# A hybrid recurrent/gating block on one core: three engine lists of its recurrent units in another order, and two weight sums made earlier on POOL

## The chip, the cores and the metric

The kernel runs on one core of one Trainium2 chip. The metric is the device time of one execution in microseconds; 1542.42 us is the median of three executions before the change (1542.19 to 1542.64).

## The reference

One layer over a sequence of 1024 tokens with 1024 channels (batch 1), all in fp32:

```python
h = modulated_rmsnorm(x, g, shift1, scale1)
xr, gr, zu, zv, ga, gb = split(h @ w_in)                  # six times 1024 columns
xr = causal_dwconv(xr, rnn_conv_w, rnn_conv_b)            # 4 taps
r = sigmoid(block_diag(xr, w_a) + b_a)                    # 8 heads of 128 x 128
i = sigmoid(block_diag(xr, w_x) + b_x)
log_a = 8 * r * log_sigmoid(lam);  a = exp(log_a)
u = sqrt(-expm1(2 * log_a)) * (i * xr)
hs = scan(h_t = a_t * h_t-1 + u_t)                        # along the sequence
y_a = (hs * gelu(gr)) @ w_branch_a
y_b = (gelu(zu) * position_mix(layernorm(gelu(zv)))) @ w_branch_b
x = x + gate1 * ((sigmoid(ga) * y_a + sigmoid(gb) * y_b) @ w_out)
h = modulated_rmsnorm(x, g2, shift2, scale2)              # then up-projection, conv(3), gelu(a)*b,
x = x + gate2 * (ffn(h) @ w_down)                         # down-projection, and a last rmsnorm
```

## The kernel before

**Units.** The work is a list `SEQ` of units, each of which makes two tiles of 128 x 1024 in PSUM (a "value" and an "activation" tile). The list begins G0, G1 (gates), then R0 to R7 (the recurrent units, one for each head), ZV0 to ZV3, G2 to G7, ZU0 to ZU3, and then the branches, the output projection and the channel sub-layer. `pos` is a unit's place in the list: R0 to R7 are pos 2 to 9, ZV0 and ZV1 are pos 10 and 11. The change touches the loops over pos 2 to 19.

**Products.** Most units are computed by a Strassen-like scheme with seven products instead of eight: b11, t1, t2, b22, t3, b21 and t4, in this order on TensorE (L807, called from `unit`). Each product is 12 matmuls of 128 x 128 by 128 x 512, because an fp32 operand is split into a high and a low part of fp32r and three partial products are taken. After the fourth product of pos, the block-diagonal matmuls of the recurrent unit before it (L930, 12 matmuls) go between.

**Weight operands.** Op n of a unit (n0 to n0+6 in the order A11, S1, S2, S4, S3, A12, A22) is the weight side of one product. A11, A21, A22 and A12 are loaded from HBM by the SP queue into `raw` buffers; POOL makes four of the seven operands in `weight_sums`: S1 = A21 + A22 (L649), S3 = A11 - A21 (L652), S2 = S1 - A11 (L656), S4 = A12 - S2 (L660). S1 needs a free buffer, which it gets when the low part of op n0+5 of the unit before is made. S2 overwrites A11 and so waits for the low part of op n0, and S4 overwrites S1 and waits for that of op n0+1. ScalarE then copies the operand to its high part (`hi`, L1221), VectorE subtracts to get the low part (`lo`, L1834), and the product waits for `lo` (semaphore f_lo). Loads of A21 and A22 of the next unit reuse buffers that `lo(n0+3)` of this unit frees.

**Snapshots and joins.** ScalarE copies three PSUM banks aside in a unit (`snap`, L1236, after products b11, t1 and t2), because the next product goes onto the same bank; VectorE adds them back (`join` 0, 1, 2, L1848). Product t2 waits for snap 0, b22 for snap 1, t3 for snap 2, and t4 for joins 0 and 1.

**A recurrent unit m** is finished while the products of the two units after it run. In the unit right after it: ScalarE starts the convolution (`conv_start`, L1354, still at the end of the unit itself), VectorE does three more taps (`conv`, L2011) and the low part of the block-diagonal weights (L2019), ScalarE takes the gelu (L1362) and the high part of the convolved tile (`conv_high`, L1374), VectorE its low part (`conv_low`, L2024), then TensorE does the block-diagonal product. `gate_pair` (L1382, L1387) takes the two tanh, `decay` a tanh, an exp and a square (L1394, L1398, L1403), and VectorE `gated_input` (L2029). There is one buffer `la_a` for the decay: the first tanh of unit m waits until the scan of unit m-1 has been done. In the unit after that: `decay_square` (L2034, VectorE), `decay_root` (L1407, ScalarE), `scan_input` and `scan` (L2039, L2043, VectorE), and the product with the gelu gate on POOL (L667), whose result SP stores.

**Order.** Each engine runs its own list, written out by hand as a loop over pos and seven steps w in a unit. An engine works its list strictly in order, and a wait holds up all that stands behind it. ScalarE's and VectorE's lists work on `hi(n0+w+3)` and `lo(n0+w+3)` at step w, so in steps 4 to 6 they make the first operands of the next unit: n0+7, n0+8, n0+9 are the next unit's A11, S1 and S2.

Of the kernel before, what the change touches and what calls it, by code (L numbers as in the profile page):

```python
# [17 lines left out]
def build(nc, a, out):  # L18
# [16 lines left out]
    CW = a["rnn_conv_w"].shape[1]  # L35
# [37 lines left out]
    with ExitStack() as ctx:  # L73
# [558 lines left out]
        @block.gpsimd  # L632
        def _(pool):
            nc.gpsimd.memset(ident[:, :], 0.0).then_inc(consts_made, 1)
            pool.wait_ge(consts_made, 1)
            nc.gpsimd.affine_select(out=ident[:, :], in_=ident[:, :], compare_op=ALU.not_equal, fill=1.0, base=0,
                                    pattern=[[-1, P]], channel_multiplier=1).then_inc(consts_made, 1)
            nc.gpsimd.memset(ones[:, :], 1.0).then_inc(consts_made, 1)

            def weight_sums(item, parts=(0, 1)):  # L640
                n0, at = first_op[item], s_slots[item]
                made = 4 * block_unit[item]
                a11, a21, a22, a12, s1 = (raw[at[x][0]][:, 0:depth[n0], :] for x in ("A11", "A21", "A22", "A12", "S1"))
                if 0 in parts:
                    if at["S1"][1] is not None:
                        pool.wait_ge(f_lo, at["S1"][1] + 1)
                    pool.wait_ge(at["A21"][1], at["A21"][2])
                    pool.wait_ge(at["A22"][1], at["A22"][2])
                    nc.gpsimd.tensor_tensor(s1, a21, a22, ALU.add).then_inc(s_made, 1)  # L649
                    pool.wait_ge(at["A11"][1], at["A11"][2])  # L650
                    pool.wait_ge(s_made, made + 1)
                    nc.gpsimd.tensor_tensor(a21, a11, a21, ALU.subtract).then_inc(s_made, 1)  # L652
                if 1 in parts:
                    pool.wait_ge(f_lo, n0 + 1)
                    pool.wait_ge(s_made, made + 2)
                    nc.gpsimd.tensor_tensor(a11, s1, a11, ALU.subtract).then_inc(s_made, 1)  # L656
                    pool.wait_ge(f_lo, n0 + 2)
                    pool.wait_ge(at["A12"][1], at["A12"][2])
                    pool.wait_ge(s_made, made + 3)
                    nc.gpsimd.tensor_tensor(s1, a12, a11, ALU.subtract).then_inc(s_made, 1)  # L660

            for pos in range(2, AT["A", 0]):
                weight_sums(SEQ[pos])
                m = prev_unit(pos, "R", 2)
                if m is not None:
                    pool.wait_ge(scanned, m + 1)
                    nc.gpsimd.tensor_tensor(ti[m % 2][:, :], ti[m % 2][:, :], gg[m % 2][:, :], ALU.mult).then_inc(y_ready, 1)  # L667
                if SEQ[pos] == ("ZV", 0):
                    pool.wait_ge(ws_landed, 16)
                    nc.gpsimd.affine_select(out=ws_raw[:, :, :], in_=ws_raw[:, :, :], compare_op=ALU.is_ge, fill=0.0, base=0,  # L670
                                            pattern=[[0, G], [-1, P]], channel_multiplier=1).then_inc(ws_masked, 1)

            weight_sums(("O", 2))

            for pos in range(NF + PLAIN, len(SEQ) - 1):
                if SEQ[pos][0] != "M":
                    weight_sums(SEQ[pos])


            for i in range(2 * KT - 1):  # L680
                h = i // KT
                pool.wait_ge(sqf_ready, i + 1)
                if i % KT == 0:
                    pool.wait_ge(sum_lo, IN_LO + O_PARTS + 4)
                    nc.gpsimd.tensor_copy(qf[:, H[h]], sqf[i % 4][:, :]).then_inc(qf_added, 1)
                else:
                    pool.wait_ge(qf_added, i)
                    nc.gpsimd.tensor_tensor(qf[:, H[h]], qf[:, H[h]], sqf[i % 4][:, :], ALU.add).then_inc(qf_added, 1)
# [524 lines left out]
        def _(act):  # L1213
# [176 lines left out]
            def decay(m, weights, n):  # L1390
                act.wait_ge(gates_read, 2 * m + 1)
                if m:
                    act.wait_ge(m2_ready, m)
                nc.scalar.activation(th[:, :], la_a[:, :], ACT.Tanh, bias=la4n[:, m:m + 1],  # L1394
                                     scale=la4n[:, m:m + 1]).then_inc(ach, 1)
                weights(n)
                act.wait_ge(ach, 2 * m + 1)
                nc.scalar.activation(la_a[:, :], la_a[:, :], ACT.Exp, bias=la4[:, m:m + 1],  # L1398
                                     scale=la4[:, m:m + 1]).then_inc(ach, 1)
                act.wait_ge(ach, 2 * m + 2)  # L1400
                if m:
                    act.wait_ge(tail_step, m)
                nc.scalar.activation(m2[:, :], la_a[:, :], ACT.Square).then_inc(th_ready, 1)  # L1403

            def decay_root(m):
                act.wait_ge(m2_ready, m + 1)
# [59 lines left out]
            for pos in range(2, AT["A", 0]):  # L1466
# [2 lines left out]
                m, m_past = prev_unit(pos, "R"), prev_unit(pos, "R", 2)  # L1469
                b = V_BLOCK[pos] if pos in V_BLOCK else None  # L1470
                for w in range(7):
                    if w in (1, 2, 3):
                        snap(pos, w - 1)
                    if m is not None and w == 2:
                        conv_high(m)
                    if w == 0:
                        if m is not None:
                            block_diag_high(m)
                        elif pos > 2:
                            OUT[SEQ[pos - 1][0]](pos - 1, 1)  # L1480
                        if SEQ[pos] == ("G", 2):
                            stage(0)
# [336 lines left out]
        def _(dve):  # L1819
# [184 lines left out]
            lo(10)  # L2004


            def conv(m, banks):
                x, src = xc[m % 2], flat(banks[0])
                dve.wait_ge(tap0, m + 1)
                for d in range(1, CW):  # L2010
                    tap = V.scalar_tensor_tensor(x[:, d:S], src[:, 0:S - d], C("rnn_conv_w", (CW - 1 - d) * KT + m), x[:, d:S],  # L2011
                                                 ALU.mult, ALU.add)
                    if d < CW - 1:
                        step(tap)
                tap.then_inc(conv_done, 1)

            def block_diag_low(m):
# [68 lines left out]
            for pos in range(2, AT["A", 0]):  # L2086
# [3 lines left out]
                b = V_BLOCK[pos] if pos in V_BLOCK else None  # L2090
                past = BANKS[(pos - 1) % 2]
                for w in range(7):
                    if w >= 4:
                        join(pos, w - 4)
                    if m is not None and w == 5:
                        gated_input(m)
                    if m is not None:
                        if w == 0:
                            conv(m, past)
                            block_diag_low(m)  # L2100
                        if w == 1:
                            conv_low(m)
                    if m_past is not None and w == 1:
                        decay_square(m_past)
                    if m_past is not None and w == 3:
                        scan_input(m_past)
                        scan(m_past)
# [19 lines left out]
                    if item == ("ZU", 3):  # L2127
                        for k in ((), (), (), (0, 1), (2, 3), (), (4, 5))[w]:
                            ya_low(k)
                    lo(n0 + w + 3)  # L2130


            def ada_piece(e, k):
# [562 lines left out]
```

## Time and profile before

| | |
|---|---|
| median of three executions | 1542.42 us |
| the profiled execution's own time | 1542.83 us |
| its span, first to last instruction | 1540.8 us |
| TensorE busy | 1516.1 us (98%), 6820 matmuls |
| VectorE busy | 1222.6 us (79%) |
| ScalarE busy | 811.0 us (53%) |
| POOL busy | 381.7 us (25%) |
| granted TensorE clock | 1.000 in the whole span |
| pos 4 to pos 11 (R2 to ZV1) on TensorE | 125.83 to 304.73 us |

Times are in microseconds from the first instruction. "Busy" is the time in which an engine has an instruction under way; matmuls are pipelined, so a busy TensorE can still be held up a little between two of them. Weight loads (PEld) show the pace better: each matmul has one.

### The profile page before, as it was taken

The page shows a single profiled execution, that of the slowest core. Times are in us where ns is not written, and L with a number is a line of the kernel's source. Part 1 is how long each engine was busy: PE and PEld are TensorE (multiplying, and loading weights), DVE is VectorE, ACT ScalarE, POOL GpSimd, SP SyncE. Part 2 cuts the span into 40 slices and gives each one's busy share as a digit, 9 for nine tenths or more (in the row PEclk, how much of TensorE's full clock was granted, in tenths as well). Part 3 has the DMA queues.
Part 4 walks back from the last instruction along what each step waited for, and adds up shares of the span by engine and source line. Part 5 has one row for each costly group of instructions (what it writes and reads, how often), then busy time and mean ns, then how long its engine had stood idle before and what let it go on. Part 6 is the DMA issues. An engine that isn't in the chain of part 4 may idle for free.

```text
span 1540.8 us, 19510 instructions
## 1 busy us (share of the span) xinstructions
PE 1516.1 (98%) x6820; PEld 1241.4 (81%) x6820; DVE 1222.6 (79%) x1484; ACT 811.0 (53%) x1207; POOL 381.7 (25%) x291
## 2 busy tenths in 40 slices
PE   7999999999999999999999999999999999999998
PEld 4778777788888888888887788888888888888887
DVE  6987988745656685478868999999999987778786
ACT  5368888645555461012534555555555553444447
POOL 0023434422222200000010333333333331233224
PEclk9999999999999999999999999999999999999999
DMA  9532222312332347574421144444444446677722
GB/s 347 180 105 60 89 69 79 96 55 82 106 103 66 110 150 233 181 246 146 164 62 35 48 150 161 154 150 150 151 151 151 150 130 229 229 242 252 238 89 110
DMA packets 199984, 219.56 MB, mean 142 GB/s; under 512 B 8944, under 2 KB 155728, under 8 KB 199120
## 3 DMA queue, kind: packets, MB, share of 16 engines
q1 hardware_dynamic: 199888, 218.32, 42.8%
q8 instruction: 55, 0.90, 0.2%
q14 instruction: 41, 0.34, 0.1%
HBM read 160.61 MB, written 57.67 MB: 142 GB/s over the span
## 4 chain that ended last, share of the span: by engine, by line
PE 76%; DVE 15%; ACT 4%; issue 3%; DMA 1%; POOL 0%; SPq 0%; ACTq 0%; DVEq 0%; POOLq 0%
PE ps L807 57%; PE ps L880 10%; DVE wop L1834 4%; DVE hidw L2466 1%; PE ps L1158 1%; PE ps L1067 1%; PE ps L1010 1%; PE ps L1140 1%; DVE ps L1848 1%; PE ps L965 1%; DVE part_acc L1897 1%; ACT wop L1221 1%; DVE yq L1932 1%; DVE tn L1927 1%; DVE ti L2039 1%
## 5 line engine op out<-in xcount | busy, mean ns | idle before, releaser
L1221 ACT ACTIVATE wop<-raw 128x512 fp32r<-128x512 f32 (+1 forms) x529 | 299.8, 570 | 419.2 <-PE ps L807 162.0
L1834 DVE TENSOR_TENSOR wop<-raw,wop 128x512 fp32r<-128x512 f32 (+1 forms) x529 | 385.5, 736 | 165.1 <-ACT wop L1221 161.8
L807 PE MATMUL ps<-yq,wop 128*128 128x512 f32 x1680 | 405.2, 390 | 1.3 <-DVE wop L1834 0.7
L807 PEld LDWEIGHTS ps<-yq,wop 128*128 128x128 f32 x1680 | 314.3, 188 | 71.2 <-issue 3.9
L649 POOL TENSOR_TENSOR raw<-raw,raw 128x512 f32<-128x512 f32 (+1 forms) x65 | 96.4, 1483 | 863.3 <-DVE wop L1834 377.5
L807 PE MATMUL ps<-dq,wop 128*128 128x512 f32 x840 | 191.3, 389 | 0.5 <-DVE wop L1834 0.5
L807 PEld LDWEIGHTS ps<-dq,wop 128*128 128x128 f32 x840 | 157.4, 188 | 34.2 <-issue 1.2
L807 PE MATMUL ps<-t4q,wop 128*128 128x512 f32 x528 | 128.5, 392 | 2.0 <-DVE ps L1848 1.9
L807 PE MATMUL ps<-t2q,wop 128*128 128x512 f32 x528 | 127.7, 391 | 1.8 <-DVE wop L1834 1.0
L807 PE MATMUL ps<-t3q,wop 128*128 128x512 f32 x528 | 127.9, 391 | 0.8 <-ACT snap_u L1236 0.8
L807 PE MATMUL ps<-t1q,wop 128*128 128x512 f32 x528 | 127.7, 391 | 0.0
L1848 DVE TENSOR_TENSOR ps<-ps,snap_p 128x512 f32<-128x512 f32 x128 | 88.8, 694 | 47.3 <-PE ps L807 46.6
L2466 DVE SCALAR_TENSOR_TENSOR hidw<-ps,pc,hidw 128x1023 f32<-128x1023 f32 x96 | 122.5, 1277 | 0.9
L1236 ACT ACTIVATE snap_p<-ps 128x512 f32<-128x512 f32 x128 | 76.3, 596 | 83.2 <-PE ps L807 82.8
L807 PEld LDWEIGHTS ps<-t4q,wop 128*128 128x128 f32 x528 | 98.2, 188 | 26.6 <-DVE ps L1848 6.5
L807 PEld LDWEIGHTS ps<-t2q,wop 128*128 128x128 f32 x528 | 98.8, 188 | 23.7 <-ACT snap_p L1236 3.1
L807 PEld LDWEIGHTS ps<-t3q,wop 128*128 128x128 f32 x528 | 98.4, 188 | 21.5 <-ACT snap_u L1236 1.2
L807 PEld LDWEIGHTS ps<-t1q,wop 128*128 128x128 f32 x528 | 98.5, 188 | 20.1
L656 POOL TENSOR_TENSOR raw<-raw,raw 128x512 f32<-128x512 f32 (+1 forms) x65 | 79.6, 1224 | 75.3 <-DVE wop L1834 71.0
L660 POOL TENSOR_TENSOR raw<-raw,raw 128x512 f32<-128x512 f32 (+1 forms) x65 | 75.6, 1163 | 78.9 <-DVE wop L1834 73.9
L652 POOL TENSOR_TENSOR raw<-raw,raw 128x512 f32<-128x512 f32 (+1 forms) x65 | 88.0, 1354 | 9.3
L880 PE MATMUL ps<-ya_split,wop 128*128 128x512 f32 x384 | 87.8, 390 | 0.0
(266 smaller groups left out, 1978.9 us busy)
## 6 DMA issues: line engine op xcount, KB each, us to landing
dq<-hid_keep SPq DMA_DIRECT2D x35, 1024.0 KB, 7.3
raw<-in_w_in SPq DMA_DIRECT2D x96, 256.0 KB, 3.3
raw<-in_w_up SPq DMA_DIRECT2D x96, 256.0 KB, 3.3
hid_keep<-part_b SPq DMA_DIRECT2D x40, 512.0 KB, 3.0
ada_ring<-in_w_ada SPq DMA_DIRECT2D x32, 512.0 KB, 4.6
hid_keep<-part_t SPq DMA_DIRECT2D x20, 512.0 KB, 2.8
raw<-in_w_down SPq DMA_DIRECT2D x80, 128.0 KB, 2.4
ada_w<-in_w_ada SPq DMA_DIRECT2D x8, 1024.0 KB, 11.5
```

The lines of the kernel that those rows point to most:

```text
L649: nc.gpsimd.tensor_tensor(s1, a21, a22, ALU.add).then_inc(s_made, 1)
L652: nc.gpsimd.tensor_tensor(a21, a11, a21, ALU.subtract).then_inc(s_made, 1)
L656: nc.gpsimd.tensor_tensor(a11, s1, a11, ALU.subtract).then_inc(s_made, 1)
L660: nc.gpsimd.tensor_tensor(s1, a12, a11, ALU.subtract).then_inc(s_made, 1)
L807: done = nc.tensor.matmul(bank, left[:, w, lk, :], right[:, x, rk, :], start=(first and w == 0 and x == 0), stop=(last and w == 1), skip_g ...
L880: done = nc.tensor.matmul(psum[:, h, :], wop[n % 4][:, w, k % KH, :], right(k, x, h), start=(k == 0 and w == 0 and x == 0), stop=(k == KT ...
L965: last = nc.tensor.matmul(blocks(past[1])[:, g, :], vhat[:, g, :], wsT[:, g, :], start=True, stop=True)
L1221: nc.scalar.activation(wop[n % 4][:, 0, 0:depth[n], :], raw[slot][:, 0:depth[n], :], ACT.Copy).then_inc(f_hi, 1)
L1236: nc.scalar.activation(dst[:, :], src, ACT.Copy).then_inc(snapped, 1)
L1834: V.tensor_tensor(wop[n % 4][:, 1, 0:kd, :], raw[slot_of[n][0]][:, 0:kd, :], wop[n % 4][:, 0, 0:kd, :].bitcast(F32), ALU.subtract).then_in ...
L1848: V.tensor_tensor(out_b, in_b, kept[:, :], ALU.add).then_inc(joined, 1)
L2466: tap = V.scalar_tensor_tensor(dst[:, d:S], src[:, 0:S - d], C("ffn_conv_w01" if k < 2 else "ffn_conv_w2", k % 2 * 2 * FT + f), dst[:, d:S ...
```

## The change

Four things change in the loops over pos 2 to 19:

- POOL: while recurrent units are in flight, S1 and S3 of the next unit are made before the gate product (L667) of this step instead of after it.
- ScalarE, `decay`: `hi(n0+8)` stands behind the square instead of between tanh and exp.
- ScalarE, unit ZV1 alone: snapshot 0 stands before the second gelu of ZV0 instead of two instructions behind it.
- VectorE, where a recurrent unit precedes: `lo(n0+3)` stands between the second and the third of the convolution's taps; joins 0 and 1 stand together ahead of `lo(n0+7)`; join 2 stands ahead of `lo(n0+8)`; `decay_square(m)` is moved from step 1 of the next unit to step 6 of this one, between `lo(n0+8)` and `lo(n0+9)`.

```diff
             for pos in range(2, AT["A", 0]):
-                weight_sums(SEQ[pos])
                 m = prev_unit(pos, "R", 2)
+                weight_sums(SEQ[pos], (1,) if prev_unit(pos, "R", 3) is not None else (0, 1))
                 if m is not None:
+                    weight_sums(SEQ[pos + 1], (0,))
                     pool.wait_ge(scanned, m + 1)
                     nc.gpsimd.tensor_tensor(ti[m % 2][:, :], ti[m % 2][:, :], gg[m % 2][:, :], ALU.mult).then_inc(y_ready, 1)
...
                 nc.scalar.activation(th[:, :], la_a[:, :], ACT.Tanh, bias=la4n[:, m:m + 1],
                                      scale=la4n[:, m:m + 1]).then_inc(ach, 1)
-                weights(n)
                 act.wait_ge(ach, 2 * m + 1)
                 nc.scalar.activation(la_a[:, :], la_a[:, :], ACT.Exp, bias=la4[:, m:m + 1],
                                      scale=la4[:, m:m + 1]).then_inc(ach, 1)
...
                 nc.scalar.activation(m2[:, :], la_a[:, :], ACT.Square).then_inc(th_ready, 1)
+                weights(n)
...
                 for w in range(7):
-                    if w in (1, 2, 3):
+                    if w in (1, 2, 3) and (w > 1 or SEQ[pos] != ("ZV", 1)):
                         snap(pos, w - 1)
...
                     if w == 0:
+                        if SEQ[pos] == ("ZV", 1):
+                            snap(pos, 0)
...
-            def conv(m, banks):
+            def conv(m, banks, weights, n):
                 x, src = xc[m % 2], flat(banks[0])
                 dve.wait_ge(tap0, m + 1)
                 for d in range(1, CW):
+                    if d == CW - 1:
+                        weights(n)
+                        dve.wait_ge(vch, middle)
                     tap = V.scalar_tensor_tensor(x[:, d:S], src[:, 0:S - d], C("rnn_conv_w", (CW - 1 - d) * KT + m), x[:, d:S],
                                                  ALU.mult, ALU.add)
-                    if d < CW - 1:
+                    if d < CW - 2:
                         step(tap)
+                    elif d == CW - 2:
+                        middle = step_number(tap)
                 tap.then_inc(conv_done, 1)
...
                 for w in range(7):
-                    if w >= 4:
+                    if w == 4 or w >= 4 and m is None:
                         join(pos, w - 4)
-                    if m is not None and w == 5:
-                        gated_input(m)
                     if m is not None:
+                        if w == 4:
+                            join(pos, 1)
+                        if w == 5:
+                            gated_input(m)
+                            join(pos, 2)
+                        if w == 6:
+                            decay_square(m)
                         if w == 0:
-                            conv(m, past)
+                            conv(m, past, lo, n0 + 3)
                             block_diag_low(m)
                         if w == 1:
                             conv_low(m)
-                    if m_past is not None and w == 1:
-                        decay_square(m_past)
...
-                    lo(n0 + w + 3)
+                    if w or m is None:
+                        lo(n0 + w + 3)
```

## Rows read from the trace of the kernel before

**Rows 1.** The page: the span and the chain that ended last.
```profile
span 1540.8 us, 19510 instructions
...
PE 76%; DVE 15%; ACT 4%; issue 3%; DMA 1%; POOL 0%; SPq 0%; ACTq 0%; DVEq 0%; POOLq 0%
```

**Rows 2.** Timeline of the weight loads: start, length, operation, [idle before].
```profile
192.60 2.68 PEld L807 LDWEIGHTS ps<-yq,wop 128*128 128x128 f32 x12
195.32 2.68 PEld L807 LDWEIGHTS ps<-t1q,wop 128*128 128x128 f32 x12
...
201.28 2.58 PEld L807 LDWEIGHTS ps<-yq,wop 128*128 128x128 f32 x12 [0.56 <-issue]
...
212.47 2.59 PEld L807 LDWEIGHTS ps<-t4q,wop 128*128 128x128 f32 x12 [0.45 <-DVE ps L1848]
215.10 2.68 PEld L807 LDWEIGHTS ps<-yq,wop 128*128 128x128 f32 x12
...
290.57 2.61 PEld L807 LDWEIGHTS ps<-t2q,wop 128*128 128x128 f32 x12 [1.06 <-ACT snap_p L1236]
...
302.05 2.63 PEld L807 LDWEIGHTS ps<-t4q,wop 128*128 128x128 f32 x12 [0.71 <-DVE ps L1848]
```

**Rows 3.** Timeline of ScalarE in the unit at pos 7.
```profile
195.89 0.63 ACT L1221 ACTIVATE wop<-raw 128x512 fp32r<-128x512 f32 x1
...
200.27 1.06 ACT L1374 ACTIVATE xc_split<-xc 128x1024 fp32r<-128x1024 f32 x1
...
203.75 1.06 ACT L1407 ACTIVATE m<-m 128x1024 f32<-128x1024 f32 x1 [0.61 <-DVE m L2034]
...
208.44 1.12 ACT L1382 ACTIVATE la_a<-ps,hba 128x1024 f32<-128x1024 f32 x1 [0.80 <-DVE ti L2043]
...
212.99 0.63 ACT L1221 ACTIVATE wop<-raw 128x512 fp32r<-128x512 f32 x1 [1.30 <-POOL raw L649]
...
214.79 1.06 ACT L1403 ACTIVATE m<-la_a 128x1024 f32<-128x1024 f32 x1
216.39 1.21 ACT L1354 ACTIVATE xc<-ps,pc 128x1024 f32<-128x1024 f32 x1 [0.54 <-DVE ps L1848]
```

**Rows 4.** Timeline of VectorE in the same unit.
```profile
196.33 3.90 DVE L2011 SCALAR_TENSOR_TENSOR xc<-ps,pc,xc 128x1023 f32<-128x1023 f32 x3
...
201.36 1.23 DVE L2024 TENSOR_TENSOR xc_split<-xc,xc_split 128x1024 fp32r<-128x1024 f32 x1 [0.19 <-ACT xc_split L1374]
202.50 1.22 DVE L2034 SCALAR_TENSOR_TENSOR m<-m,th 128x1024 f32<-128x1024 f32 x1
203.64 1.29 DVE L1834 TENSOR_TENSOR wop<-raw,wop 128x512 fp32r<-128x512 f32 x2
...
204.85 1.23 DVE L2039 TENSOR_TENSOR ti<-ti,m 128x1024 f32<-128x1024 f32 x1
206.11 2.29 DVE L2043 TENSOR_TENSOR_SCAN ti<-la_a,ti 128x1024 f32<-128x1024 f32 x1
...
209.50 2.30 DVE L1834 TENSOR_TENSOR wop<-raw,wop 128x512 fp32r<-128x512 f32 x1
...
211.73 0.69 DVE L1848 TENSOR_TENSOR ps<-ps,snap_p 128x512 f32<-128x512 f32 x1
212.33 1.70 DVE L2029 SCALAR_TENSOR_TENSOR ti<-ti,xc 128x1024 f32<-128x1024 f32 x1
213.96 1.78 DVE L1834 TENSOR_TENSOR wop<-raw,wop 128x512 fp32r<-128x512 f32 x1
```

**Rows 5.** Timeline of POOL in the same unit.
```profile
208.48 2.78 POOL L667 TENSOR_TENSOR ti<-ti,gg 128x1024 f32<-128x1024 f32 x1 [12.62 <-DVE ti L2043]
...
213.10 2.10 POOL L652 TENSOR_TENSOR raw<-raw,raw 128x512 f32<-128x512 f32 x1
...
217.06 1.29 POOL L660 TENSOR_TENSOR raw<-raw,raw 128x512 f32<-128x512 f32 x1 [0.17 <-POOL raw L656]
```

**Rows 6.** The page's DMA issues: count, size, us to landing.
```profile
raw<-in_w_in SPq DMA_DIRECT2D x96, 256.0 KB, 3.3
```

## The prediction

> **What bounds the kernel now.** I read the page first. The span is 1540.8 us and TensorE holds three quarters of the chain that ended last [rows 1]: the kernel is a row of products, and a change pays only where a product is made to wait. So I went to the weight loads of TensorE over pos 3 to 12. Two products follow each other at 2.72 us where nothing holds them [rows 2], so the eight products of a recurrent unit could take 8 x 2.72 = 21.76 us. From pos 5 to pos 10 a unit takes 22.50 us (192.60 to 215.10 [rows 2]; the other five lie within 0.05 of it). The 0.74 us come from two waits that the reader sees there: b22 starts late at 201.28, waiting for its low weights, and t4 at 212.47, waiting for join 1. At ZV1 (pos 11) t2 waits 1.06 us for snapshot 0 and t4 0.71 us for join 1 [rows 2]. All that lists can win here is thus 6 x 0.74 = 4.4 us and some 2 us in ZV1, about 6.5 us or 0.4%.
>
> Next I asked why the waits are the same in each unit: something goes round with a period of 22.50 us. The timeline of ScalarE shows it. The first tanh of unit m waits for the scan of unit m-1 (0.80 us idle at 208.44 [rows 3]); from that tanh the list runs on without a rest through exp, square, conv_start, gelu, conv_high and root, the root releases scan_input and scan, and the scan the next tanh. This **loop** sets the period, not TensorE. Four idle times lie on it [rows 3]: 1.30 us before hi(n0+8) (it waits for S1 from POOL, and the exp is queued behind it), 0.54 before conv_start (join 2), 0.61 before the root (decay_square), and the scan itself.
>
> The timelines of VectorE and POOL show one more thing: the two engines stop each other. `lo` takes 0.69 us alone (two of them in a row 1.29 at 203.64), but 2.30 at 209.50, beside POOL's gate product, and 1.78 at 213.96 beside S3 [rows 4, 5]. Both end 0.54 us after the POOL instruction (211.80 against 211.26, 215.74 against 215.20): a held `lo` begins 0.15 before POOL is done. It works the other way too: S3 takes 2.10 instead of 1.29, ending 1.17 after gated_input (214.03) [rows 4, 5]. And it goes by turns: the `lo` at 213.96 was ready when gated_input ended, but S3 had stood waiting and went first. The join at 211.73, which has one operand in PSUM, keeps its 0.69 beside S1.
>
> **The change, part by part.** I follow the loop once round. Let s be the end of the square.
>
> *Taken out of the loop.* hi(n0+8) no longer stands in front of the exp, so its 1.30 goes. Join 2 is ahead of lo(n0+8) and done long before conv_start: 0.54 goes. decay_square is done a unit earlier, so the root runs as soon as its table is there: 0.61 goes. Together 2.45 us. Also b22 gets lo(n0+3) one tap earlier, and t4 gets join 1 ahead of the `lo` that the gate product held (2.30). If nothing else happened, the loop would be 20.05 us, and TensorE with 21.76 would set the pace.
>
> *S4 behind decay_square.* hi(n0+8) now starts at the end of the square (s - 0.10) and ends at s + 0.53; lo(n0+8) ends at s + 1.26. S4 overwrites S1 and waits for just this `lo`. But decay_square is next on VectorE, its square is done, and it starts before POOL has seen the semaphore: it runs from s + 1.17 to s + 2.39, and S4 ends 1.17 later, at s + 3.56. ScalarE comes to hi(n0+3), which copies S4, at s + 2.43: conv_start at s + 0.43, and 2.00 from there (216.39 to 195.89 + 22.50 [rows 3]). It waits 1.17 us. If S4 went first this would shrink to 0.2, but decay_square would push the taps back by as much, so the sum with the next item stays between 1.7 and 2.0.
>
> *The taps.* lo(n0+9) is held by S4 and ends 0.54 after it, s + 4.10. The three taps take 3.90 and lo(n0+3) among them another 0.60 [rows 4]: the convolution ends at s + 8.5. ScalarE would be at conv_high 4.38 after hi(n0+3) [rows 3], at s + 7.98. It waits 0.58 us. Behind it stand hi(n0+5) and the root. The new wait inside the convolution (for hi(n0+3), done at s + 4.2, two taps before its turn) costs nothing.
>
> *S1 ahead of the gate product.* Let x be the end of conv_high (201.33 [rows 3]). conv_low follows at once, then, with decay_square gone from here, the two `lo`: lo(n0+5) ends at x + 2.46 (0.03 + 1.14 + 1.29 [rows 4]). It frees S1's buffer and POOL starts S1 0.08 later (the lag of 208.48 behind the scan's end [rows 4, 5]); 1.29 long, it ends at x + 3.83. The loads are there: lo(n0+3) frees their buffers at s + 7.2, and 3.3 us [rows 6] later, s + 10.5, is 1.6 before S1's turn. scan_input is ready at x + 2.91 (the root starts at 203.75 - 0.61 = x + 1.81, takes 1.06). It finds S1 at work and starts at x + 3.68: 0.77 us late.
>
> *S3 ahead of the scan.* S3 has queued meanwhile and by turns goes next: scan_input ends at x + 4.91, S3 at x + 6.08, and the scan starts at x + 5.93 instead of x + 4.94: 0.99 us late. No row shows the scan beside POOL. Its price is between 0 (if it is not held) and 0.99; of the rows, it is nearest to gated_input, also 1024 long with both operands in SBUF, which was held. I take 0.99. [...]
>
> *Sum.* 22.50 - 2.45 + 1.17 + 0.58 + 0.77 + 0.99 = 23.56 us: the loop becomes longer by about 1.0 us a unit, since the two sums that POOL now makes early fall just on scan_input and scan, the only place in the loop where VectorE works alone. TensorE's waits move: t2 late for snapshot 0, b22 for snapshot 1, t4 for join 1.
>
> The loop must first eat the lead that the cuts give at its start: pos 4 stays at 21.8, pos 5 gains 0.3 over its 22.50; pos 6 to 10 lose 5 x 1.0. In ZV1 the early snapshot saves the 1.06, but t4 waits for join 1, behind scan, S3 and the product: 1.0 and about 1.3 later. Between -1.1 (the sums come after the scan) and +2.3 I take +0.4. Total 0.3 + 5.0 + 0.4 = 5.7 us. On the profiled execution (1542.83, 0.4 above the median) that is 1548.5; on the median **1548.1 us**, 0.37% slower. A change of 0.2% (3.1 us) is about what a measurement here can tell from none.
>
> **Rivals.** *1. The scan is not held by POOL.* Place: L2043 beside L652; price 0.99 a unit; it decides if the scan's mean stays at 2.29. Then the loop is 22.6, as before, but starts with its lead: about 1 us won in the first two units, perhaps 0.2 in each later one, and 1.1 in ZV1: 3 us faster, 1539.4. For it: no row shows the scan held. Against: every two-operand SBUF instruction beside POOL is. 14%.
>
> *2. S1 comes later than scan_input* (by late loads, or because the two, 0.37 apart, change places). Then S1 holds the scan alone, 1.0 instead of 1.76, and S3 comes after it; the gate product is later, in no one's way until the next sums. The loop is 22.8, ZV1 wins 0 to 1: +1 to +3.5 us, about 1544.7. Against: a margin of 1.6 us for the loads. 15%.
>
> *3. The lists do all they can:* no collision, TensorE sets the pace at 21.76; 6.5 us faster, 1536. It needs three of the four new waits to be wrong. 4%.
>
> *4. Worse:* the S1/S3 lag goes on into join 0 and 1 and the loads: 24 a unit, 1551 or more. 6%.
>
> **How the numbers follow.** The forecast (1545.5 to 1550.5, which lets the new waits sum to 2.9 to 3.7 and ZV1 go either way) has 61%. Rival 1 lies on the border and goes half to faster, half to same; rival 2 half to same, half to slower. Faster: 7 + 4 and some for what I have not seen, 16%. Same: 7 + 8 and some, 17%. Slower: 67%. The range takes in rival 2 and the upper part of rival 1: 1540.0 to 1550.5.
>
> **What the changed profile would show.** Right: weight loads of b11 about 23.4 apart from pos 6 to 10; scan_input at a mean near 2.0 instead of 1.23 and the scan near 3.2 instead of 2.29; S1 starting 0.1 after lo(n0+5); ScalarE idle some 1.1 before hi(n0+3), waiting for L660, and some 0.5 before conv_high; no idle time before exp or root; t4 of ZV1 waiting some 2 to 3 us. Wrong: a scan of 2.29 with S3 under it, S1 starting behind scan_input, or a period at or under 22.5.

## The result, and the profile after

The changed kernel takes 1548.27 us (median of five, 1544.93 to 1550.04), the kernel before 1542.42 (five, 1541.86 to 1542.64). The ratio is 1.0035, 95% interval 1.0025 to 1.0046: 5.9 us slower. (Three executions of 2182 to 3364 us, one of e1 and two of the kernel before beside it, are slow ones and stand in no comparison below.) The profiled execution took 1548.27 us, its span is 1546.3 against 1540.8 [rows 1]. VectorE was busy 1229.8 us instead of 1222.6, POOL 392.5 instead of 381.7, with the same numbers of instructions: both do the same work and hold each other up for longer.

The timeline of the weight loads shows where the 5.5 us of span lie. In order of time: the loads of b11, the first product of a unit, at pos 6, 7, 8, at ZV1 and behind it, and between them the loads that wait at pos 7 and in ZV1:

```profile
170.16 2.68 PEld L808 LDWEIGHTS ps<-yq,wop 128*128 128x128 f32 x12
193.48 2.68 PEld L808 LDWEIGHTS ps<-yq,wop 128*128 128x128 f32 x12
...
199.39 2.62 PEld L808 LDWEIGHTS ps<-t2q,wop 128*128 128x128 f32 x12 [0.51 <-ACT snap_p L1237]
202.73 2.63 PEld L808 LDWEIGHTS ps<-yq,wop 128*128 128x128 f32 x12 [0.73 <-ACT snap_p L1237]
...
214.18 2.63 PEld L808 LDWEIGHTS ps<-t4q,wop 128*128 128x128 f32 x12 [0.63 <-DVE ps L1851]
216.85 2.68 PEld L808 LDWEIGHTS ps<-yq,wop 128*128 128x128 f32 x12
...
286.82 2.68 PEld L808 LDWEIGHTS ps<-yq,wop 128*128 128x128 f32 x12
...
307.36 2.61 PEld L808 LDWEIGHTS ps<-t4q,wop 128*128 128x128 f32 x12 [3.36 <-DVE ps L1851]
310.01 2.68 PEld L808 LDWEIGHTS ps<-yq,wop 128*128 128x128 f32 x12
```

From pos 6 to 10 a unit takes (286.82 - 170.16) / 5 = 23.33 us instead of 22.50 [rows 2], in all 4.2 us more. ZV1 takes 23.19 instead of 22.14 (1.05 more). Pos 4 and 5 gain 0.04 and 0.18. That is 5.03 in all; with 0.25 ahead of pos 4 and 0.22 behind ZV1 it makes up the 5.5. The two waits of before (b22 for its low weights, t4 for join 1 [rows 2]) are now three: t2 and b22 for snapshots, t4 for join 1.

ScalarE in the same unit, beside [rows 3]:

```profile
198.22 0.63 ACT L1222 ACTIVATE wop<-raw 128x512 fp32r<-128x512 f32 x1 [1.12 <-POOL raw L660]
...
203.07 1.06 ACT L1375 ACTIVATE xc_split<-xc 128x1024 fp32r<-128x1024 f32 x1 [0.39 <-DVE xc L2017]
...
205.97 1.06 ACT L1408 ACTIVATE m<-m 128x1024 f32<-128x1024 f32 x1
...
212.37 1.12 ACT L1383 ACTIVATE la_a<-ps,hba 128x1024 f32<-128x1024 f32 x1 [2.52 <-DVE ti L2051]
...
215.65 1.25 ACT L1398 ACTIVATE la_a<-la_a,la 128x1024 f32<-128x1024 f32 x1
216.93 1.06 ACT L1403 ACTIVATE m<-la_a 128x1024 f32<-128x1024 f32 x1
217.90 0.61 ACT L1222 ACTIVATE wop<-raw 128x512 fp32r<-128x512 f32 x1
218.41 1.19 ACT L1355 ACTIVATE xc<-ps,pc 128x1024 f32<-128x1024 f32 x1
```

The idle times of before ahead of exp, conv_start and root are gone. In their place ScalarE waits 1.12 us for S4 and 0.39 for the convolution, and the first tanh waits 2.52 instead of 0.80 for the scan. Why the scan is late shows when VectorE and POOL are read together (beside [rows 4, 5]), first VectorE, then POOL:

```profile
207.06 1.98 DVE L2047 TENSOR_TENSOR ti<-ti,m 128x1024 f32<-128x1024 f32 x1 [0.47 <-ACT m L1408]
209.07 3.26 DVE L2051 TENSOR_TENSOR_SCAN ti<-la_a,ti 128x1024 f32<-128x1024 f32 x1
...
218.54 0.69 DVE L1837 TENSOR_TENSOR wop<-raw,wop 128x512 fp32r<-128x512 f32 x1 [1.08 <-ACT wop L1222]
219.15 1.22 DVE L2042 SCALAR_TENSOR_TENSOR m<-m,th 128x1024 f32<-128x1024 f32 x1
220.29 1.78 DVE L1837 TENSOR_TENSOR wop<-raw,wop 128x512 fp32r<-128x512 f32 x1
```
```profile
206.67 1.29 POOL L649 TENSOR_TENSOR raw<-raw,raw 128x512 f32<-128x512 f32 x1 [8.48 <-DVE wop L1837]
208.10 2.09 POOL L652 TENSOR_TENSOR raw<-raw,raw 128x512 f32<-128x512 f32 x1
212.41 2.76 POOL L668 TENSOR_TENSOR ti<-ti,gg 128x1024 f32<-128x1024 f32 x1 [2.23 <-DVE ti L2051]
...
219.31 2.20 POOL L660 TENSOR_TENSOR raw<-raw,raw 128x512 f32<-128x512 f32 x1 [1.30 <-DVE wop L1837]
```

S1 runs when scan_input becomes ready, which so takes 1.98 us instead of 1.23. S3 is in turn held by scan_input (2.09) and ends at 210.19; the scan, under way on paper from 209.07, ends 2.14 later, at 212.33. The hold shows as length, not as idle time. Over all eight recurrent units (rows by form, mean ns of one), before 2292 and 1226 (the 1894 is made of seven times some 1990 and, in ZV1, 1226):

```profile
L2051 DVE TENSOR_TENSOR_SCAN ti<-la_a,ti 128x1024 f32<-128x1024 f32 x8 | 26.1, 3263 | 0.3
L2047 DVE TENSOR_TENSOR ti<-ti,m 128x1024 f32<-128x1024 f32 x8 | 15.2, 1894 | 4.9 <-ACT m L1408 4.9
```

### The profile page after: what moved, and what is told of

It is laid out like the page before. It is cut to its first block, busy times and chain, and to the rows that moved or that the text cites. A ratio compares the mean times of both kernels' runs of the same rounds, so it can differ in the third digit from the quotient of the medians.

```text
span 1546.3 us, 19510 instructions
## 1 busy us (share of the span) xinstructions
PE 1517.5 (98%) x6820; PEld 1241.3 (80%) x6820; DVE 1229.8 (80%) x1484; ACT 811.2 (52%) x1207; POOL 392.5 (25%) x291
## 4 chain that ended last, share of the span: by engine, by line
PE 74%; DVE 15%; ACT 5%; issue 3%; DMA 1%; POOL 1%; SPq 0%; ACTq 0%; DVEq 0%; POOLq 0%
PE ps L808 55%; PE ps L881 10%; DVE wop L1837 3%; DVE hidw L2478 1%; DVE xc L2017 1%; PE ps L1159 1%; PE ps L1068 1%; PE ps L1011 1%; DVE ti L2051 1%; PE ps L1141 1%; PE ps L966 1%; ACT wop L1222 1%; DVE ti L2047 1%; DVE part_acc L1900 1%; DVE yq L1935 1%
## 5 line engine op out<-in xcount | busy, mean ns | idle before, releaser
L649 POOL TENSOR_TENSOR raw<-raw,raw 128x512 f32<-128x512 f32 (+1 forms) x65 | 92.5, 1424 | 932.2 <-DVE wop L1837 438.6
L656 POOL TENSOR_TENSOR raw<-raw,raw 128x512 f32<-128x512 f32 (+1 forms) x65 | 83.8, 1289 | 83.2 <-DVE wop L1837 80.2
L660 POOL TENSOR_TENSOR raw<-raw,raw 128x512 f32<-128x512 f32 (+1 forms) x65 | 82.9, 1276 | 84.4 <-DVE wop L1837 80.5
L652 POOL TENSOR_TENSOR raw<-raw,raw 128x512 f32<-128x512 f32 (+1 forms) x65 | 90.9, 1398 | 9.3
```

## The experiments

Theory: the loop of the prediction. POOL's early sums hold scan_input and scan, S4 comes late behind decay_square, and this costs more than the three removed waits give. Rivals: the lists alone are the loss; the scan isn't what costs; only the end, ZV1, costs. Here a unit, and ZV1, is measured from the start of its second product, t1, to that of the next unit: 23.29 to 23.38 in pos 6 to 10 and 23.15 in ZV1 after, 22.45 to 22.52 and 22.14 before.

### Each part alone

POOL's order of before in the changed kernel:

```diff
+                weight_sums(SEQ[pos])
                 m = prev_unit(pos, "R", 2)
-                weight_sums(SEQ[pos], (1,) if prev_unit(pos, "R", 3) is not None else (0, 1))
                 if m is not None:
-                    weight_sums(SEQ[pos + 1], (0,))
...
```

> The changed VectorE and ScalarE lists with POOL's order of before. Theory (four waits in the loop through the scan: S4 behind decay_square, the taps, S1 against scan_input, S3 against the scan): the last two go, so scan_input and scan are back at 1.23 and 2.29, but hi(n0+8) again waits for S1 behind the gate product, and S4 still stands behind decay_square; following the durations of the rows once round gives about 23.2 us a unit, some 3.6 us slower than before in all, 1546. Rival A (only POOL's early sums cost, the lists by themselves gain): under 22.0 a unit, 1538 to 1540. Rival B (only the lists cost): 23.3 as with the whole change, 1547 to 1548.

Measured: 1546.29 us, ratio 1.0023 (1.0013 to 1.0034); units of 23.04 to 23.47. The scan is back at 2291 ns and scan_input at 1225, as expected, and still the unit is 0.7 over that of before. ScalarE now waits twice for POOL, which makes S1, S3, S2 and S4 in a row after the product. The waits are for S2 and S4, not for S1 as I had expected: `hi(n0+8)` now stands behind the square, and S1 is done by then (timeline of ScalarE in this run):

```profile
218.24 0.63 ACT L1221 ACTIVATE wop<-raw 128x512 fp32r<-128x512 f32 x1 [1.03 <-POOL raw L656]
...
220.47 0.63 ACT L1221 ACTIVATE wop<-raw 128x512 fp32r<-128x512 f32 x1 [1.29 <-POOL raw L660]
```

The other half: the kernel before, with POOL's new order and nothing else.

```diff
-                weight_sums(SEQ[pos])
                 m = prev_unit(pos, "R", 2)
+                weight_sums(SEQ[pos], (1,) if prev_unit(pos, "R", 3) is not None else (0, 1))
                 if m is not None:
+                    weight_sums(SEQ[pos + 1], (0,))
...
```

> The lists of before with POOL's new order alone. Theory: the collisions of S1 and S3 with scan_input and scan (1.76 a unit) stay, none of the waits that the lists take out of the loop goes but the one for S1 (1.30), and join 1 stays behind the low part that the gate product holds: about 23.9 a unit already from pos 4, 8 to 9 us slower than before, 1551. Rival A (POOL's order costs what the whole change costs): 23.3 a unit, 1547 to 1548. Rival B (only the lists cost): 22.5 or less, 1540 to 1542.

Measured: 1552.60 us, ratio 1.0064 (1.0048 to 1.0080); units of 23.80 to 23.87, the scan at 3265 ns. The period is near the expected 23.9, but not by the expected sum: S1 waits for a load, comes behind scan_input (which keeps a mean of 1298 ns) and holds the scan alone. ScalarE no longer waits for S1 ahead of the exp, but 2.11 instead of 0.54 for join 2 ahead of conv_start (timeline of ScalarE in this run):

```profile
221.18 1.21 ACT L1355 ACTIVATE xc<-ps,pc 128x1024 f32<-128x1024 f32 x1 [2.11 <-DVE ps L1849]
```

So 22.50 + 0.97 - 1.30 + 1.57 = 23.74. Join 2 is late since gated_input and two `lo` ahead of it are late. Each part alone loses (0.7 and 1.4 us a unit) and together they lose 0.84, so the losses don't add up. In the whole change conv_start doesn't wait for join 2, which the lists have moved ahead; that this is what takes the sum below the two parts is argued, not shown by a run of its own.

### Which of the new waits costs

S1 stays ahead of the scan, S3 goes behind the gate product (in this edit part 3 of `weight_sums` is S3 alone, and part 0 is S1 alone):

```diff
                     nc.gpsimd.tensor_tensor(ti[m % 2][:, :], ti[m % 2][:, :], gg[m % 2][:, :], ALU.mult).then_inc(y_ready, 1)
+                    weight_sums(SEQ[pos + 1], (3,))
...
```

> The changed kernel, but S3 is made behind the gate product again; S1 stays ahead of it. Theory: S3 no longer queues between scan_input and scan; the scan's mean falls from 3.26 to 2.3, scan_input stays near 2.0; the unit falls from 23.33 to about 22.9 (S3 later collides with other VectorE work), the whole to 1.9 us over before, 1544. Rival A (the scan's 3.26 has another cause): scan stays at 3.2 and the unit at 23.3.

Measured: 1545.59 us, ratio 1.0017 (1.0008 to 1.0027); units of 22.78 to 22.86 from pos 7 on (22.26 at pos 6, where the lead of the first units ends). POOL and VectorE of this run at pos 7:

```profile
204.81 1.30 POOL L649 TENSOR_TENSOR raw<-raw,raw 128x512 f32<-128x512 f32 x1 [8.48 <-DVE wop L1839]
209.59 2.77 POOL L669 TENSOR_TENSOR ti<-ti,gg 128x1024 f32<-128x1024 f32 x1 [3.49 <-DVE ti L2053]
```
```profile
205.20 1.99 DVE L2049 TENSOR_TENSOR ti<-ti,m 128x1024 f32<-128x1024 f32 x1 [0.47 <-ACT m L1410]
207.22 2.29 DVE L2053 TENSOR_TENSOR_SCAN ti<-la_a,ti 128x1024 f32<-128x1024 f32 x1
```

With no sum beside it the scan takes 2.29 again: in these units S3 alone was its hold. (In ZV1 of this run the scan still reads 3.28, beside S1; see below.) The unit falls by 0.53, not by 0.97. The rest, 0.44, is given back: hi(n0+3), waiting for S4, comes 9.62 us after the first tanh (219.17 - 209.55) instead of 9.18 (221.55 - 212.37), with gated_input now held by S3 (2.31 instead of 1.21). The total is 1.6 us above the expected 1544; ZV1 took 25.07 in its profile (below).

decay_square back where it was:

```diff
-                        if w == 6:
-                            decay_square(m)
...
+                    if m_past is not None and w == 1:
+                        decay_square(m_past)
```

> The changed kernel, but decay_square stands where it stood before (step 1 of the next unit, behind conv_low). Theory: S4 follows lo(n0+8) at once, ScalarE's 1.12 us of idle time before hi(n0+3) falls to about 0.2, but the root waits for decay_square again (about 0.6): 22.8 a unit, 2.6 us over before in all, 1545. Rival A (S4 is late for another reason): idle before hi(n0+3) stays near 1.1 and the unit gets 0.6 longer, 23.9.

Measured: 1545.23 us, ratio 1.0018 (1.0008 to 1.0027); units of 22.61 to 22.66. The wait for S4 falls from 1.12 to 0.45, while the root waits 0.60 again. The root is then late enough that scan_input starts ahead of S1 and keeps its 1226 ns; now S1 is held (2.22), and then holds the scan (3265 ns).

`lo(n0+3)` back behind the third tap:

```diff
-                    if d == CW - 1:
-                        weights(n)
-                        dve.wait_ge(vch, middle)
...
                 tap.then_inc(conv_done, 1)
+                weights(n)
```

> The changed kernel, but lo(n0+3) stands behind the third tap again (and ahead of the low part of the block-diagonal weights). Theory: the taps end 0.6 earlier, conv_high does not wait for them, and the loop gets shorter by that 0.4 to 0.6 us a unit, 22.8; the product b22 does not need the earlier low part, since its wait is for snapshot 1. About 1 us over before, 1543. Rival A (the early lo(n0+3) is what the change wins at b22, as its wait before the change suggests): b22 waits longer and the unit is 23.3 to 23.8.

Measured: 1543.90 us, ratio 1.0005 (0.9996 to 1.0015); units of 22.46 to 22.72, the scan at 3142 ns in the mean. The total can no longer be told from that of the kernel before. Rival A is out: b22 waits for snapshot 1, not for its weights. So this one `lo` between the taps, meant to give b22 its weights sooner, cost 0.6 to 0.9 us a unit, in two ways. The convolution was late: conv_high's wait of 0.39 is gone. The rest goes by S1, which waits for the loads that this `lo` frees: from pos 5 on S1 now starts 0.44 us or more behind scan_input, which so keeps its 1.23 us, and S1 holds the scan alone. At pos 7 it began only at 205.99, when the scan was under way, and the scan took 2.29.

ScalarE's list: the ninth cast back between tanh and exp.

```diff
                 nc.scalar.activation(th[:, :], la_a[:, :], ACT.Tanh, bias=la4n[:, m:m + 1],
                                      scale=la4n[:, m:m + 1]).then_inc(ach, 1)
+                weights(n)
...
                 nc.scalar.activation(m2[:, :], la_a[:, :], ACT.Square).then_inc(th_ready, 1)
-                weights(n)
```

> The changed kernel, with ScalarE's ninth cast back between the tanh and the exponential, where the kernel before had it. Theory A (POOL's S4 makes that cast late, by the 1.12 us measured at the third cast, so putting it back where nothing of the loop waits for S4 takes that wait out of the loop but gives back what the removed waits had won): units of about 22.7 us, 1543.5. Theory B (the cast between tanh and exponential stands 1.30 us in the loop, as in the kernel before, and the wait for S4 stays elsewhere): units above 23.3 us, 1549 or more.

Measured: units of 22.59 to 22.88, as A has it, and 1545.14 us (1541.46 to 1546.60), ratio 1.0014 (1.0005 to 1.0024), 1.6 over what A had: its ZV1 took 24.78 (below). With S1 made early the cast has nothing to wait for ahead of the exp and takes its 0.62 alone. Behind the square it is late for lo(n0+8), which waits 1.08 in the changed kernel, and S4 waits for that `lo`. Back in its place, that wait is gone and the one for S4 is 0.61 instead of 1.12 (timeline of ScalarE in this run):

```profile
218.68 0.63 ACT L1222 ACTIVATE wop<-raw 128x512 fp32r<-128x512 f32 x1 [0.61 <-POOL raw L660]
```

Once S1 is early, moving the cast behind the square costs 0.64 a unit in the mean.

### ZV1 and the uneven times

The changed kernel varied by 5.1 us, the one before by 0.8 (and by 2.3 over the 29 executions beside the last runs). In ZV1, S1 of ZV2 had to wait for a load and started only 0.5 ahead of the scan, behind scan_input (timelines of after, POOL and then VectorE):

```profile
298.52 1.63 POOL L649 TENSOR_TENSOR raw<-raw,raw 128x512 f32<-128x512 f32 x1 [6.77 <-DMA raw<-in_w_in]
300.30 3.09 POOL L652 TENSOR_TENSOR raw<-raw,raw 128x512 f32<-128x512 f32 x1
303.35 2.79 POOL L668 TENSOR_TENSOR ti<-ti,gg 128x1024 f32<-128x1024 f32 x1
```
```profile
299.03 3.27 DVE L2051 TENSOR_TENSOR_SCAN ti<-la_a,ti 128x1024 f32<-128x1024 f32 x1
302.23 1.71 DVE L1837 TENSOR_TENSOR wop<-raw,wop 128x512 fp32r<-128x512 f32 x1
303.86 0.69 DVE L1851 TENSOR_TENSOR ps<-ps,snap_u 128x512 f32<-128x512 f32 x1
304.46 2.23 DVE L1837 TENSOR_TENSOR wop<-raw,wop 128x512 fp32r<-128x512 f32 x1
306.62 0.69 DVE L1851 TENSOR_TENSOR ps<-ps,snap_p 128x512 f32<-128x512 f32 x1
```

The order is thus another than at pos 4 to 10. scan_input keeps its 1.23 and holds S1 (1.63); S1 ends at 300.15 and holds the scan, which ends 2.15 later, at 302.30. S3 is in turn held by the scan (3.09), and holds the `lo` of 1.71; the gate product holds the `lo` of 2.23, and join 1 (306.62) stands behind all of them. The two expectations below say that S3 holds the scan in ZV1. These rows show S1, and in e3, where S3 stands behind the gate product, the scan of ZV1 reads 3.28 all the same.

The scan of unit 7 put behind join 1, in ZV1 alone:

```diff
                         scan_input(m_past)
+                        if m is not None:
+                            scan(m_past)
+                    if m_past is not None and m is None and w == 5:
                         scan(m_past)
```

> The changed kernel, with the scan of unit 7 put behind join 1 in ZV1's step alone; every other unit as it was. Theory (in ZV1 the scan is held by S3 of ZV2, and join 1 behind it lets TensorE stand 3.36 us): ZV1 takes about 20 us instead of 23.19, the units ahead of it keep their 23.3, and the time falls by some 3 us to about 1545. If the uneven times of the changed kernel (1544.9 to 1550.0) come from the order in which ZV1's scan and S1 of ZV2 start, they are now within about 2 us of each other. Rival (what follows ZV1 only shifts, so the scan is paid there): ZV1 is shorter, the next unit longer by as much, and the time stays at 1548 with its spread.

Measured: 1544.83 us, ten executions within 1544.14 to 1545.52; ratio 1.0014 (1.0005 to 1.0023). ZV1 took 19.89, the next unit 0.2 more, the units ahead kept their 23.3. The rival, that it only shifts, is out. Beside it the changed kernel itself:

> The changed kernel itself, run again. Theory: a median near 1548, times that again differ by several us, while those of the kernel before beside it stay within 2 us; ZV1 in its profile takes either about 23.2 us (S1 of ZV2 starts ahead of the scan, which S3 then holds) or about 1.5 us less (the scan starts first).

Measured: 1546.86 us (eight, 1545.10 to 1549.58), ratio 1.0030 (1.0020 to 1.0041). The median came out 1.1 below the expected 1548, and those of the kernel before beside it spread over 2.3 us, not 2. All 13 times of this kernel have the median 1547.78 and fall in two groups, five from 1544.93 to 1546.12 and eight from 1547.61 to 1550.04. The profiled execution (1549.36 us) agrees with neither form that I expected: the scan is held (3.27) and t4 waits 3.34, as in the first profile, but ZV1 took 24.75. The loads of t4 and of the next b11, on the timeline of this execution:

```profile
307.30 3.62 PEld L808 LDWEIGHTS ps<-t4q,wop 128*128 128x128 f32 x12 [3.34 <-DVE ps L1851]
311.02 3.22 PEld L808 LDWEIGHTS ps<-yq,wop 128*128 128x128 f32 x12
```

The same stretch by windows (window, its length, busy time of PE, PEld, VectorE, ScalarE, POOL, then the granted clock as a share, the share of the DMA engines and GB/s):

```profile
307.30:309.00 1.70, 1.70 (x7) 1.36 (x8) 1.70 (x2) 0.94 (x2) 1.07 (x2) 0.91 0.98 308
309.00:311.00 2.00, 2.00 (x6) 1.54 (x5) 1.46 (x2) 1.99 (x2) 0.91 (x1) 0.50 0.77 271
311.00:312.70 1.70, 1.70 (x7) 1.37 (x6) 0.00 (x0) 1.03 (x3) 0.00 (x0) 0.67 0.18 52
```

TensorE had stood for 3.34 us, ran again, and was then granted 0.50 of its clock; the two products took 1.0 and 0.5 us longer than in the profile after. In the first profile it had stood 3.36 us, and the clock stayed at 1.00 in all these windows. What makes the clock fall is thus not shown: the stand was as long in both. The 1.5 us between these two executions agree with the clock in the windows, an estimate: 0.09 x 1.70 + 0.50 x 2.00 + 0.33 x 1.70 = 1.7 us.

The fall is the rule here, and the first profile the exception. In e3, e4, e5, e6 and e11, too, t4 of ZV1 stood for 2.74 to 3.32 us, the clock went to 0.50 in the stand or shortly behind it, and t4's loads took 3.67 to 4.77 us instead of 2.61. In e7, e8 and e9 t4 waits for nothing, and the clock stays at 1.00. The totals of the kernels with the stand spread over 3.5 to 5.1 us, that of e9 over 1.4, so the lengths of the units say more about the lists than the totals do.

The clock does not make the lower group: the first profile has no fall and took 1548.27 us. Nor do the mean clocks on record tell the groups apart (0.998 to 1.000 in the lower, 0.998 or 0.999 in the upper). That the lower group is made of executions in which the scan starts ahead of S1 fits e9's 1544.83 us, but none of them was profiled: it is argued only.

### What the lists can win

The kernel before with one swap, decay_square ahead of conv_low:

```diff
-                        if w == 1:
-                            conv_low(m)
                     if m_past is not None and w == 1:
                         decay_square(m_past)
+                    if m is not None:
+                        if w == 1:
+                            conv_low(m)
```

> The kernel before, with one swap in VectorE's list: decay_square of the past unit ahead of conv_low, as in the change. POOL and ScalarE untouched. Theory (decay_square is ready long before conv_low, so that conv_low's wait for ScalarE's split is filled): units of about 22.2 us instead of 22.5, and some 2.8 us less in all, 1539.7. Rival (the swap only delays conv_low, and with it the square root's chain): units of 22.5 or more, no change.

Measured: 1540.08 us, ratio 0.9985 (0.9975 to 0.9994); units of 22.11 to 22.24, the root no longer waits. The changed kernel with the same idea, decay_square of the past unit behind the convolution, on top of e5's edit:

```diff
-                        if w == 6:
-                            decay_square(m)
...
                             conv(m, past, lo, n0 + 3)
+                            if m_past is not None:
+                                decay_square(m_past)
                             block_diag_low(m)
+                    elif m_past is not None and w == 1:
+                        decay_square(m_past)
...
```

> The changed kernel with two edits: lo(n0+3) behind the third tap, and decay_square of the past unit between lo(n0+3) and the low part of the block-diagonal weights, ahead of conv_low. Theory: S4 no longer stands behind decay_square, the root no longer waits for it, the taps are on time; of the four new waits S1 and S3 against scan_input and scan are left (1.76), against 2.45 won: 22.0 a unit. ZV1's t4 still waits some 3 us for join 1. In all 2.5 us under before, 1540. Rival A (the collisions with the scan alone carry the loss): 22.8 a unit or more, not under before.

Measured: 1541.10 us, ratio 0.9990 (0.9981 to 1.0000); units of 21.76 to 21.93, though the scan is held in each (3262 ns). The loop now goes round in 21.89 us (scan_input at 181.03, 202.91 and 224.80), only 0.13 above TensorE's 21.76: a held scan costs little once the other waits are out of the loop. ZV1 took 25.95: a held scan there and, behind it, t4 in 4.77 instead of 2.68 us, at a granted clock of 0.50. Three edits more, e9's and these two (the gelu goes ahead of hi(n0+3)):

```diff
                         if m is not None:
+                            gate_gelu(pos - 1)
                             block_diag_high(m)
...
-                    if w == 1 and m is not None:
-                        gate_gelu(pos - 1)
...
+                            join(pos, 2)
                             gated_input(m)
-                            join(pos, 2)
...
```

> The two edits of the run before and three more: the gelu ahead of hi(n0+3) in ScalarE's list (it can run while hi(n0+3) would wait), join 2 ahead of gated_input, and in ZV1 the scan behind join 1. Theory: nothing in the loop is longer than TensorE's own 21.76, the waits on TensorE vanish from pos 4 to ZV1 and t4 of ZV1 does not wait: 7 to 8 us under before, 1535. Rival A (another resource closes the loop at about 22): 1538 to 1540.

Measured: 1536.98 us, ratio 0.9961 (0.9946 to 0.9975), 5.6 under the kernel before beside it (1542.58) and not 7 to 8. The theory failed in one point: the loop goes round in 22.10 us (scan_input at 179.81, 201.92 and 224.02), as rival A had it, and once the lead is used up the units take 22.09 and 22.11 (pos 9 and 10), with t2 waiting 0.46 for snapshot 0. The time lies below rival A's 1538 because the lead lasts to pos 8 and ZV1 takes 19.93. In these rounds VectorE is recorded busy for 21.69 of 22.10 us: the instructions that POOL's early sums hold nearly fill it. Last, the kernel before, POOL and `decay` untouched, with five moves in the lists (decay_square, joins 0 and 1, join 2, the gelu, and ZV1's snapshot 0):

```diff
+                        if SEQ[pos] == ("ZV", 1):
+                            snap(pos, 0)
                         if m is not None:
+                            gate_gelu(pos - 1)
                             block_diag_high(m)
...
+                    early = m is not None or item == ("ZV", 1)
+                    if w >= 4 and not (early and w == 5):
+                        join(pos, w - 4) if not (m is not None and w == 6) else None
+                    if early and w == 4:
+                        join(pos, 1)
                     if m is not None and w == 5:
+                        join(pos, 2)
                         gated_input(m)
...
```

The first part is ScalarE's list, the second VectorE's, where e10's swap is made too.

> The kernel before with POOL's and decay's order untouched, and four edits: decay_square ahead of conv_low, joins 0 and 1 together ahead of lo(n0+7) (in ZV1 too), join 2 and gated_input ahead of lo(n0+8), the gelu ahead of hi(n0+3) and the early snapshot of ZV1. Theory: the early sums on POOL are not needed; the loop falls under 21.76 without them: 7 to 8 us under before, 1535, as the run before. Rival A (the wait for S1 before the exp, 1.30 a unit, must go first): 22.0 to 22.5 a unit, 1538 to 1542.

Measured: 1536.03 us, ratio 0.9955 (0.9941 to 0.9970). Every unit from pos 4 to 10 takes 21.76, ZV1 19.93, and TensorE waits nowhere in them. VectorE, with the sums of POOL where they were before, is busy for 18.62 of 21.77 us (scan_input at 201.11 to the next at 222.88). TensorE's loads at pos 7, and the scan:

```profile
207.10 2.68 PEld L807 LDWEIGHTS ps<-yq,wop 128*128 128x128 f32 x12
209.82 2.68 PEld L807 LDWEIGHTS ps<-t4q,wop 128*128 128x128 f32 x12
212.54 2.68 PEld L807 LDWEIGHTS ps<-yq,wop 128*128 128x128 f32 x12
```
```profile
202.37 2.29 DVE L2044 TENSOR_TENSOR_SCAN ti<-la_a,ti 128x1024 f32<-128x1024 f32 x1
```

It is faster than both kernels, by 6.55 us than the one before beside it (1542.58). That is the 6.5 us which the prediction named as all that lists can win, and a little under the 7 to 8 expected of this run. Rival A is out: ScalarE still waits 0.77 us for S1 ahead of the exp, and the unit takes 21.76 all the same.

## Why the prediction was right, step by step

- **The loop through scan, tanh, exp, square, conv_start, conv_high, root and scan_input sets the period.** Shown: with the rows of after, 22.50 - 2.45 + 1.12 + 0.39 + 0.75 + 0.97 = 23.28, measured 23.33.
- **Three waits go (1.30, 0.54, 0.61).** All three, in after. But the 1.30 is not the cast's alone to give: with S1 early it goes without moving the cast, and moving it costs 0.64 (e11). The prediction had one removal for two edits and didn't see that the second makes S4 late by way of lo(n0+8).
- **S4 behind decay_square, 1.17.** 1.12 measured. S4 starts 0.16 after decay_square, ends 1.14 after it.
- **Taps, 0.58.** 0.39 measured: the convolution ended 0.13 sooner, at s + 8.37, and ScalarE was ready 0.04 later, at s + 8.02. The sign held, and e5 shows that this `lo` is a loss.
- **S1 over scan_input, 0.77, and S3 over the scan, 0.99.** 0.75 and 0.97. Rival 1 (the scan is not held) is out: 3.26 with S3 beside it, 2.29 in e3 with S3 moved. That the scan is held as gated_input is (1.70 in [rows 4]) was the author's estimate; no row of before shows it, and the 3.26 of after does.
- **Rival 2 (S1 behind scan_input, by late loads)** didn't come about in pos 4 to 10 of after, where S1 waits for the `lo` alone. It did in ZV1, where S1 waits for a load: the margin of 1.6 us for the loads, worked out for the other units, does not hold there. With other edits it came about in e4 and e5 too, at units of 22.6 and about 22.5 to 22.7 against the 22.8 that it was given.
- **The sum by stretches, 0.3 + 5.0 + 0.4 = 5.7 us.** Measured 5.03 over the same stretch, 5.5 with what lies ahead and behind. Three terms were mis-sized: pos 5 won 0.18 instead of losing 0.3; a unit of pos 6 to 10 lost 0.84 instead of 1.0, through the taps and S4; ZV1 lost 1.05 instead of 0.4, in an execution of the upper group, and by S1 in front of the scan. The first two made the sum too long by 1.3, the third too short by 0.65. With ZV1's scan out of the way (e9) the total would have been 2.4 us, still slower. That 1548.1 came within 0.2 us of the median of 1548.27 is in part luck: errors of 1.3 and 0.65 went against each other, and the median depends on how many executions fall in each group (1546.86 in e12, 1547.78 over all 13). What was right is the loop and its price a unit, 0.84 against 1.0.
- **Not foreseen:** that the time is no single number. The order in ZV1 hangs on 0.5 us, and behind the stand of some 3 us there the granted clock fell to 0.50 in six of the seven profiles that show it.

## What to carry to other kernels

Ask of work moved on POOL what VectorE does in its new place: here two instructions that read two SBUF operands each ran in turn, so a sum that leaves a join in PSUM at its 0.69 us (before, beside S1) cost 0.75 us beside scan_input, and another 0.97 beside the scan. Find the loop that goes round through all engines, and move out of it first what is ready long before its turn; an edit that merely shortens a wait which another edit already removes can make a third party late. Here a few swaps that touch no sum gave all that TensorE's pace allows in these units.

## What the runs showed of the hardware

- A held VectorE instruction reads longer: the scan of 2.29 us reads 3.26 with S3 in front, and ends 2.14 after S3 does; with S1 in front (ZV1) it reads 3.27 and ends 2.15 after S1. The same goes for POOL: S1 of 1.29 reads 2.22 in e4, S3 up to 3.10.
- Turns decide by tenths: in after S1 starts 0.39 ahead of scan_input and holds it; in e4 scan_input starts 0.15 ahead of S1 and holds that.
- TensorE stood for 3.34 us and for 3.36 us at the same place in two executions; the clock fell to 0.50 in the first and not in the second. In e3 it fell after a stand of 2.74 us (0.74, 0.50 and 0.94 in the three windows of some 2 us after it). Of seven profiles with such a stand, six show the fall.
